# The FFN down-projection of a decoder step as seven half-size products, their operands formed by adding DMAs

## What is computed

```python
def conv_ffn(x, hist, g, w_up, cw, cb, w_down):
    h = rms_norm(x, g)
    u = jnp.einsum('btd,df->btf', h, w_up)
    ext = jnp.concatenate([hist.astype(u.dtype), u], axis=1)
    T = u.shape[1]
    c = cb + sum(cw[j] * ext[:, j: j + T] for j in range(CONV_W))
    a, b = jnp.split(c, 2, axis=-1)
    out = jnp.einsum('btf,fd->btd', jax.nn.silu(a) * b, w_down)
    return out, ext[:, -(CONV_W - 1):]
```

## Time and profile before

| | |
|---|---|
| median of 3 runs | 2337.22 us (2330.64 to 2339.39) |
| the profiled execution: device time | 2330.3 us |
| its span, first to last instruction | 2328.5 us |
| PE, DVE, ACT, POOL busy | 2240.7, 1543.4, 989.5, 228.4 us |
| mean granted TensorE clock | 0.977 of full |
| HBM read, written | 226.64, 69.72 MB |

### The profile page before, as it was taken

One profiled execution on the slowest core, in us unless ns is written; L12 is line 12 of the kernel. 1 busy time (PEld: TensorE's weight loads), 2 busy tenths in 40 slices (PEclk: granted clock), 3 DMA queues, 4 the chain that ended last, 5 costly groups with the idle time before them and its releaser, 6 DMA issues.

```text
span 2328.5 us, 46067 instructions
## 1 busy us (share of the span) xinstructions
PE 2240.7 (96%) x17352; PEld 2186.1 (94%) x17363; DVE 1543.4 (66%) x2401; ACT 989.5 (42%) x1870; POOL 228.4 (10%) x329
## 2 busy tenths in 40 slices
PE   7899999999999999999999998879999999999999
PEld 7899999998999999999999886578999999989999
DVE  5778888887455566364462776566888888864445
ACT  5544445455344433132231543354554444543333
POOL 1000000000011045152341220010000000000000
PEclk8899999999999999999999999898999999999999
DMA  6122222224654622322222796531222222255555
GB/s 197 64 65 81 81 73 72 81 83 166 243 171 142 216 80 79 97 85 92 72 82 93 238 295 184 172 132 55 65 80 81 81 78 75 87 218 198 189 185 161
DMA packets 204887, 290.39 MB, mean 125 GB/s; under 512 B 14343, under 2 KB 145719, under 8 KB 204498
## 3 DMA queue, kind: packets, MB, share of 16 engines
q1 hardware_dynamic: 199970, 284.00, 37.4%
q10 hardware_dynamic: 4792, 4.68, 0.6%
HBM read 226.64 MB, written 69.72 MB: 127 GB/s over the span
## 4 chain that ended last, share of the span: by engine, by line
PE 88%; DVE 5%; DMA 2%; ACT 2%; issue 1%; SPq 0%; ACTq 0%; POOL 0%; DVEq 0%; POOLq 0%
PE ps L1200 37%; PE ps L1289 20%; PE ps L1885 6%; PE ps L1883 6%; PE ps L1884 6%; PE ps L394 3%; PE ps L2121 2%; PE ps L2094 1%; PE ps L2105 1%; PE ps L2061 1%; PE ps L2133 1%; PE ps L826 1%; PE ps L452 1%; DMA om<-os_ 1%; PE ps L1880 1%
## 5 line engine op out<-in xcount | busy, mean ns | idle before, releaser
L1200 PE MATMUL ps<-hT,w 128*128 128x258 f32 x2752 | 462.9, 285 | 3.7 <-DVE w L1042 2.3
L1200 PEld LDWEIGHTS ps<-hT,w 128*128 128x128 f32 x2752 | 388.8, 192 | 4.6 <-DVE w L1042 2.7
L1289 PE MATMUL ps<-gdh,whl 128*128 128x384 f32 (+1 forms) x1472 | 351.3, 320 | 0.7 <-DVE x L1499 0.7
L1200 PE MATMUL ps<-lT,w 128*128 128x258 f32 x1376 | 278.8, 284 | 0.0
L1289 PEld LDWEIGHTS ps<-gdh,whl 128*128 128x128 f32 x1472 | 255.6, 189 | 1.7 <-DVE x L1499 1.3
L1200 PE MATMUL ps<-hB,w 128*128 128x258 f32 x1344 | 230.8, 284 | 4.4 <-DVE ub L1399 4.4
L1289 PE MATMUL ps<-gdl,whl 128*128 128x384 f32 (+1 forms) x736 | 234.3, 318 | 0.0
L1200 PEld LDWEIGHTS ps<-lT,w 128*128 128x128 f32 x1376 | 215.7, 192 | 0.0
L1200 PEld LDWEIGHTS ps<-hB,w 128*128 128x128 f32 x1344 | 192.0, 191 | 4.8 <-DVE ub L1399 4.8
L1151 ACT ACTIVATE w<-sq 128x1024 fp32r<-128x1024 f32 x84 | 88.8, 1057 | 174.4 <-PE ps L1200 169.6
L1479 DVE TENSOR_TENSOR whl<-stage,whl 128x1024 fp32r<-128x1024 f32 x62 | 75.9, 1224 | 108.5 <-ACT whl L1488 108.5
(11 more groups left out here) (345 smaller groups left out, 5384.3 us busy)
## 6 DMA issues: line engine op xcount, KB each, us to landing
stage<-in_w_down SPq DMA_DIRECT2D x100, 512.0 KB, 3.6
stage<-in_w_up SPq DMA_DIRECT2D x176, 256.0 KB, 3.1
gs<-cb SPq DMA_DIRECT2D x44, 516.0 KB, 2.7
graw<-gs SPq DMA_DIRECT2D x80, 192.0 KB, 3.8
rb<-in_w_down SPq DMA_DIRECT2D x30, 512.0 KB, 3.6
stage<-in_w_kv SPq DMA_DIRECT2D x24, 512.0 KB, 4.0
kvs<-kn SPq DMA_DIRECT2D x48, 256.0 KB, 2.0
xsp<-x SPq DMA_DIRECT2D x16, 516.0 KB, 2.7
```

Of the source, the lines that this page charges most:

```text
L1200: mm = pe.matmul(ps[:, bank + c, 0:HB], w, m[:, c * HB:(c + 1) * HB], start=(first and i == 0), stop=(i == len(parts) - 1), skip_group_che ...
L1289: mm = pe.matmul(ps[:, d, 0:n], wt_, m, start=(f == 0 and i == 0), stop=(f == NF - 1 and i == 2))
```

## The change

The second phase becomes the same seven-product scheme. `w_down` is cut into its two halves of rows (11 x 128 each) and of columns (512 each), G into its two halves of rows and of tokens (516 each). Each product has 11 steps p; a step is 4 blocks d x 3 x 2 matmuls of 258 columns, in 77 steps (`NSTEPS`) per layer. Some products accumulate on the PSUM contents of the one before (`FRESH` names those that start anew); after each, DVE adds the four blocks to one quadrant of x (`add_x`; `adds_after` says after which step's low parts). Four of the seven products need sums of blocks of `w_down` (`wsum` in DRAM), and four need sums of blocks of G (`tsum` in DRAM). No engine computes these: POOL's queue issues DMAs from DRAM to DRAM, plain copies and copies that add to their destination (`accum_op`), in 26 rounds per layer, 9 a round at the most. Round `it` waits for G[it] and its negated half in DRAM, for the second half of `w_up` of step it+2, and for all DMAs of the round before. Negated halves (`gneg`) are made by one more ACT instruction a step (`negated`) and stored by SP. The conv tails at the seam come before the last silu on ACT. x comes back by quadrants.

```diff
+        PRODUCTS = ("P1", "P6", "P7", "P4", "P5", "P3", "P2")
+        NP = NF // 2
+        NSTEPS = 7 * NP
+        FRESH = (0, 4, 6)
+        TARGETS = ((0, 1), (0, 0), (1, 0), (1, 1), (1, 0), (0, 0), (0, 1))
+        QUADS = {3: 0, 4: 1, 5: 2, 6: 3}
+        RESULT_AT = {3: 0, 5: 1, 6: 2}
...
+        def paired(L, i):
+            return i == 6 or (L == 1 and i in (3, 5))
...
+        def sp_down(sp, L, S, n):
+            i, p = n // NP, n % NP
+            name, slot = PRODUCTS[i], slot_of(n)
...
+            if n >= 4:
+                sp.wait_ge(f_dl, S.dl + 2 * n - 6)
...
+            if i in (1, 3, 5):
+                sp.wait_ge(sums_in, summed(L, {1: max(NP + p + 1, 2 * p + 3), 3: NP + p + 3, 5: 2 * p + 5}[i]))
+            sp.dma_start(dwr[slot], wsrc).then_inc(f_wd_in[n % 4], 16)
...
+            sp.dma_start(dxr[slot], xsrc).then_inc(f_wd_in[n % 4], 16)
...
             def keep(f):
                 sp.wait_ge(f_prod, f + (S.prod + 1))
                 sp.dma_start(gs[L, bass.ds(f, 1)].rearrange("o p n -> p (o n)"), cb[:, :]).then_inc(f_kept, 16)
+                sp.wait_ge(f_silu_ng, 2 * f + (S.silu + 2))
+                sp.dma_start(gneg[L, bass.ds(f, 1)].rearrange("o p n -> p (o n)"), gn[:, :]).then_inc(f_kept, 16)
...
         def pe_down(pe, L, S):
-            def one(c, f, d, slot):
-                w, wt = wdh[slot][:, d * P:(d + 1) * P], wdl[slot][:, d * P:(d + 1) * P]
-                n = THIRDS[c][1]
-                for i, (wt_, m) in enumerate(three(w, wt, gdhi[slot][:, 0:n], gdlo[slot][:, 0:n])):
-                    mm = pe.matmul(ps[:, d, 0:n], wt_, m, start=(f == 0 and i == 0), stop=(f == NF - 1 and i == 2))
+            def one(n, d, last):
+                i, p, slot = n // NP, n % NP, slot_of(n)
+                cols = slice(d * P, (d + 1) * P)
+                for j, (w, m) in enumerate(three(dwh[slot][:, cols], dwl[slot][:, cols], dxh[slot], dxl[slot])):
+                    for c in range(2):
+                        mm = pe.matmul(ps[:, 2 * d + c, 0:HB], w, m[:, c * HB:(c + 1) * HB],
+                                       start=(i in FRESH and p == 0 and j == 0), stop=(last and j == 2), skip_group_check=True)
                 return mm
...
+        def act_down(act, S, n):
+            i, slot = n // NP, slot_of(n)
+            act.wait_ge(f_wd_in[n % 4], S.wd_in[n % 4] + 32 * (n // 4) + 32)
+            act.wait_ge(*((f_pr, product_done(S, NF - 1, "P5" if n < 4 else "P4")) if n < 8 else step_done(S, n - 4)))
+            nc.scalar.activation(dwh[slot], dwr[slot], ACT.Copy).then_inc(f_dh, 1)
+            nc.scalar.activation(dxh[slot], dxr[slot], ACT.Copy, scale=-1.0 if i == 1 else 1.0).then_inc(f_dh, 1)
...
+        def pool_sums(q, L, S):
+            w = a["w_down"][L]
+            def copy(dst, src):
+                q.dma_start(dst, src).then_inc(sums_in, 16)
+            def add(dst, src):
+                q.dma_start(dst, src, accum_op=ALU.add, max_dma_last_dim=4 * N).then_inc(sums_in, 16)
...
+            for it in range(SUM_ROUNDS):
+                if it < NF:
+                    q.wait_ge(f_kept, S.kept + 32 * (it + 1))
+                if it < NF - 2:
+                    q.wait_ge(f_up_in[1], S.up_in + 32 * (it + 3))
+                if it or L:
+                    q.wait_ge(sums_in, summed(L, it - 1))
...
+        def adds_after(S, i):
+            return NP * (i + 1) + (1 if paired(S.L, i) else 2)
...
+            def negated(f, h):
+                act.wait_ge(f_prod, f + (S.prod + 1))
+                nc.scalar.activation(gn[:, :], half(cb, h), ACT.Copy, scale=-1.0).then_inc(f_silu_ng, 1)
...
                 act_copy_u3(act, S, f)
                 if not last:
                     act_high_w(act, w31[:, 0, :], sq[:, 0, 0:1024], (f_sum, sums_of(S, f + 1, "s31")))
+                    negated(f - 1, h)
                     act.wait_ge(f_pr, product_done(S, f, "P3"))
                     act_high_w(act, w24[:, 0, :], sq[:, 1, 0:1024], (f_sum, sums_of(S, f + 1, "s4")))
...
+            act_conv_tails(act, L, S, TAILS[NF, 0])
             silu(f)
-            act_conv_tails(act, L, S, TAILS[NF, 0])
+            negated(f, 1)
```

634 lines of the change are left out of this document (360 added, 274 removed).

## The result

The changed kernel takes 2351.19 us (median of 7 runs, 2343.16 to 2363.85) where the kernel before takes 2333.23 (7 runs, 2328.78 to 2339.39): a ratio of 1.0077, 95% interval 1.0051 to 1.0103. That is slower by 0.8%, where 2282 was forecast; the range given ended at 2336. The profiled execution is the one of 2351.19 us, with a span of 2349.4.

The account below looks back on a forecast made before the run. PE's count of matmuls was taken to bound both phases. Terms -56.8 + 0.5 + 1.5 - 3.0 + 3.0 gave -54.8 us, so a median of 2282 us from 2337.2, with the range 2268 to 2336 (chance 0.8).

Parts of the forecast that it names:

- Matmuls: Second phases: 1,848 matmuls of 258 columns take 221.9 us where 250.3 stood, -56.8 us for both layers.
- feeding: Second phase: loads and ACT's and DVE's parts keep up with the shorter steps of 2.88 us, cost 0.
- boundaries: Between products, PE waits for DVE's adds to x: +0.5 us for ten, +1.5 for two with layer 1's result transposes.
- seam: Between the phases, conv tail copies ahead of silu shorten PE's pause from 3.29 to 1.4 us: -1.5 per layer, -3.0.
- The end: From last product matmul to the end: copies, an add, transposes and stores take about 8 us instead of 5.0, +3.0.
- ACT's and SP's new instruction: First phase: ACT's extra 0.60 us falls in idle time and SP's extra wait delays no needed load, cost 0.
- POOL's DMAs: 176 per layer, rounds taken as 12 us: second-half w_up load stays within 7.6 us of landing, cost 0.
- late weights: Rival, first phase: POOL's packets delay w_up's second-half load, PE waits in each of 42 steps, 100 us, 2382; chance 0.11.
- smaller case: First phase: only some w_up loads late, or each by under 1.2 us; 10 to 50 us given back, about 2305; chance 0.14.
- rounds that end too late for P6: Rival: round 23 misses P6's last step if rounds exceed 15 us; at 22 us, 58 us late, 2398; chance 0.07.
- the clock out of play: PE's clock, granted in full (1.00, the 2.4 GHz level) in all three windows before, was given no term.
- DVE slowed by POOL: Rival, first phase: POOL's descriptor writing slows DVE's instructions, 2.9 us past each step, 122 us, 2404; chance 0.04.

Follow-up runs that it names:

- e1: The changed kernel without POOL's DMAs; the second phase loads w_down's own columns and gs, so sums are left out of the result: 2281.66 us, ratio 0.9782.
- e9: The changed kernel with POOL's rounds begun one load later, w_down's sums respread into smaller rounds, seam loads and adds reordered: 2291.67 us, ratio 0.9832.

## Why the prediction was wrong

By its own steps, with e1 as the kernel in which everything but POOL's DMAs is there:

- *Matmuls, -56.8; feeding 0; boundaries +0.5 and +1.5; seam -3.0*: right. Their sum for the two second phases is -57.8; e1 has 226.4 and 234.7 in place of 255.3 and 263.0, -57.2. In the change itself 1,584 matmuls ran gapless in 194.5 us, and the pause for the conv tails fell from 3.29 to 1.60 us (1.4 foretold).
- *The end, +3.0*: +3.9.
- *ACT's and SP's new instruction, 0*: right, 474.3 and 471.2 in e1 against 474.8 and 472.8.
- *POOL's DMAs, 0*: **this is the step that failed.** They cost 69.5 us between the medians; in the profiled executions 35.6 in the first phases (16.7 and 18.9 between the change and e1) and 33.5 at the seams (17.4 and 16.1). Without them, the sum holds: e1 is 53.5 us faster than the runs of the kernel before taken beside it (2335.15), where 54.8 was forecast. That e1's 2281.7 meets the 2282 to 0.3 us is luck; the median of the kernel before lay anywhere from 2331.9 to 2337.2 in its sets of runs.

The step failed in two places. In the first phase each number in it was near: the round begins about 5.5 us ahead of the load (5.0 at 376.35), it lasts 12 us (the four windows from 376 to 392 hold (0.85 + 1.06 + 1.06 + 0.42) x 4 / 1.06 = 12.8 us of full engines, the loads' own part among them), the load may take 7.6 us. But the three were not put together. I wrote that "the load sees at most the rest of a round and stays within 7.6"; the rest of a round is 12 - 5.5 = 6.5 us, and with the load's own 3.1 that is up to 9.6, over the threshold. The trace shows 8.3 to 8.9 for the rounds of seven with five or six adds, up to 13 for rounds of nine. So the rival "late weights" had the mechanism, place and threshold right (DVE idle at L1082, then L1425, then PE before `hB,w`), and lost its chance to the engines' mean share, 0.24, which says nothing of the ten microseconds after a round's start. Its price for one load was near as well: 2.4 us at 10 us of landing, where 10.12 us cost 2.04. What was too high was to have it in each of 42 steps, since of the rounds of seven only every second one passes the threshold, and by less than 1 us: 16.2 + 17.3 = 33.5 us over the kernel before is 0.8 a step. That is the "smaller case", 10 to 50 us.

At the seam, the step named a price only for rounds that end too late for P6 (15 us a round). Round 21 did take 21.4 us, but SP waited for `sums_in` only once, 2.0 us in layer 1 and without a gap on PE, where no wait was foretold. What was late is what the step didn't look at: the loads beside the last rounds. Before, loads and stores alone filled the engines at the seam (1.02); now one landing, that of the last negated store, releases nine DMAs of POOL, four x loads and eight loads of steps 8 to 11. I went through the queues for the first phase and not for the place where four of the moved pieces meet. With the first phases' 35.6 alone the time would have been about 2317; the seams' 33.5 make 2351.

The prediction also put the clock out of play, from three windows of the kernel before. In the change the gaps lower it: the mean granted clock is 0.967, against 0.980 in e1, and the cost of a gap that this adds (below) stands in no term and no price.

*DVE slowed by POOL* is false: with 99 us of POOL's issues in the first phase, DVE's sums take 1.23 us, as in the earlier trace rows, and its conv taps 1.28, as in the kernel before. The Trainium skill (SBUF — State Buffer, who interferes with whom) keeps descriptor generation, which needs the write interface, apart from the contention of reads; by that rule nothing was to be expected here, and the trace agrees.

What stays open: between e9 and e1 are 10 us, of which the stages show some 3 at each seam; the rest lies within the spread of executions (e9's own runs span 15 us) and was not followed further. Nor does any run tell whether it is the 16 engines themselves that are full at a share of 1.06 or the memory behind them.

## What to carry to other kernels

When background DMAs come in rounds, don't compare mean shares; count an adding DMA as two copies; write the round's start and length beside the issue times of the loads on the critical path, add the rest of the round to the load's own landing, and hold the sum against that load's slack. Start the round right after the load with the least slack has landed, so that the next full stretch falls on loads that have the most. And look for the one event that releases several queues together: there, shrink the background work and let no wait of the issuing queue stand ahead of loads that are due.
